# Eight prompt heads and a gelu: wider value tiles, the mask last, GpSimd for the division

## The reference

```python
z = rms_norm(x) @ w_in                      # inputs of three mixers and their gates
y_rg = RG-LRU(z)                            # conv, gates, scan
q = norm(cq @ w_uq);  latent, k_pe = ...    # 8 heads, 64 + 32 (rotary), latent of 256
s = (q_nope . k_nope + q_pe . k_pe) * ATTN_SCALE
p = softmax(where(mask, s, NEG_INF));  y_at = p @ v      # v of 64 columns a head
y_cm = gelu(u) * (w_s @ layer_norm(gelu(v)) + b_s)       # chunks of 128 tokens
x = x + (sum of gates * (y @ w_branch)) @ w_out
x = x + (silu(hf @ w_gate) * (hf @ w_up)) @ w_down
```

## Time and profile before

| | us |
|---|---|
| median of three runs | 1579.99 (1579.91 to 1580.33) |
| the profiled execution | 1581.96 |
| its span, from the first instruction to the last | 1580.0 |
| PE busy | 1550.8 (98%) |
| DVE busy | 1056.6 (67%) |
| ACT busy | 891.5 (56%) |
| POOL busy | 524.7 (33%) |

### The profile page before, as it was taken

One profiled execution on the slowest core, in us unless ns is written; L12 is line 12 of the kernel. 1 busy time (PEld: TensorE's weight loads), 2 busy tenths in 40 slices (PEclk: granted clock), 3 DMA queues, 4 the chain that ended last, 5 costly groups with the idle time before them and its releaser, 6 DMA issues.

```text
span 1580.0 us, 33275 instructions
## 1 busy us (share of the span) xinstructions
PE 1550.8 (98%) x10796; PEld 1507.2 (95%) x10796; DVE 1056.6 (67%) x1620; ACT 891.5 (56%) x1740; POOL 524.7 (33%) x709
## 2 busy tenths in 40 slices
PE   7999999999999999999999999999999999999999
PEld 7987999999999999999998789999999999999999
DVE  6777767776664766664376877777775658666633
ACT  5787776777533444443357877677764335444432
POOL 3723377676600000000048224777766001000000
PEclk9999999999999999999999999999999999999999
DMA  7331454553645444444454224545436444444443
GB/s 277 121 102 51 117 171 145 147 149 104 187 132 156 148 146 149 152 153 146 146 189 130 77 66 118 179 141 153 139 117 178 138 157 147 147 146 148 155 148 113
DMA packets 114722, 224.65 MB, mean 142 GB/s; under 512 B 12881, under 2 KB 78706, under 8 KB 114482
## 3 DMA queue, kind: packets, MB, share of 16 engines
q1 hardware_dynamic: 112178, 214.75, 44.1%
q0 software_dynamic: 2432, 8.49, 1.6%
HBM read 220.73 MB, written 2.46 MB: 141 GB/s over the span
## 4 chain that ended last, share of the span: by engine, by line
PE 81%; DVE 5%; ACT 4%; issue 3%; POOL 2%; POOLq 2%; DVEq 2%; ACTq 1%; DMA 0%; SPq 0%
PE PS L820 53%; PE PS L1075 20%; DVE w_lo L1768 1%; PE PS L1105 1%; PE PS L1106 1%; POOL r_lo L751 1%; ACT w_hi L1321 1%; POOLq L724 1%; DVEq L1762 1%; ACT r_hi L1321 1%; PE PS L876 1%; ACT lt_hi L1321 1%; PE PS L847 1%; POOL q_rot L711 0%; DVEq L2049 0%
## 5 line engine op out<-in xcount | busy, mean ns | idle before, releaser
L1768 DVE TENSOR_TENSOR w_lo<-raw,w_hi 128x1024 fp32r<-128x1024 f32 x258 | 324.9, 1260 | 221.3 <-ACT w_hi L1321 218.4
L1321 ACT ACTIVATE w_hi<-raw 128x1024 fp32r<-128x1024 f32 x258 | 272.2, 1056 | 348.6 <-PE PS L820 334.4
L820 PE MATMUL PS<-h_hi,w_hi 128*128 128x320 f32 x1360 | 425.9, 313 | 11.2 <-DVE h_lo L1795 10.4
L820 PE MATMUL PS<-h_lo,w_hi 128*128 128x320 f32 x1360 | 420.8, 309 | 0.0
L820 PE MATMUL PS<-h_hi,w_lo 128*128 128x320 f32 x1360 | 420.7, 309 | 0.0
L820 PEld LDWEIGHTS PS<-h_hi,w_hi 128*128 128x128 f32 x1360 | 255.9, 188 | 14.6 <-issue 9.6
L820 PEld LDWEIGHTS PS<-h_lo,w_hi 128*128 128x128 f32 x1360 | 256.0, 188 | 1.0
L820 PEld LDWEIGHTS PS<-h_hi,w_lo 128*128 128x128 f32 x1360 | 255.9, 188 | 0.0
L1321 ACT ACTIVATE ksqp<-PS 128x512 f32<-128x512 f32 x256 | 152.6, 596 | 135.4 <-PE PS L1075 131.6
L2109 DVE TENSOR_REDUCE kss<-ksqp 128x8 f32<-128x512 f32 x256 | 173.2, 680 | 80.5 <-ACT ksqp L1321 79.8
L1075 PE MATMUL PS<-comb_hi,lt_hi 128*128 128x288 f32 x1024 | 224.0, 300 | 3.0 <-DVE lt_lo L1771 1.5
(11 more groups left out here) (325 smaller groups left out, 2683.8 us busy)
## 6 DMA issues: line engine op xcount, KB each, us to landing
raw<-in_stream SPq DMA_DIRECT2D x258, 512.0 KB, 3.5
tpage<-in_tcache SPq DMA_DIRECT2D x256, 160.0 KB, 2.3
rrow<-in_rcache SPq DMA_DIRECT2D x256, 128.0 KB, 2.7
x<-in_xT SPq DMA_DIRECT2D x2, 640.0 KB, 7.0
sbias<-in_sbias POOLq DMA_DIRECT2D x2, 640.0 KB, 6.5
out_yT<-x SPq DMA_DIRECT2D x4, 320.0 KB, 2.2
const<-in_consts SPq DMA_DIRECT2D x1, 1090.0 KB
wgate<-in_wgate POOLq DMA_DIRECT2D x2, 512.0 KB, 4.4
```

The source lines that it names most:

```text
L820: done = mm(out, w[:, slot, c], a, start=first and n == 0 and m == 0, stop=last and n == len(pairs) - 1 and m == 2)
L1321: return nc.scalar.activation(out, in_, func, **kw)
L1768: V.tensor_tensor(w_lo[:, s, :], raw[:, s, :], f(w_hi[:, s, :]), ALU.subtract).then_inc(lo_done.sem, 1)
```

## The change

In one edit:

- The values `vp` are two tiles with 128 columns a head, 64 of them the head's and 64 zeros, placed so that a product fills all 128 partitions of the bank and two heads add up in it. GpSimd writes the zeros; ACT copies the values around them. `vp_second` lies where `wv` is loaded later, so `wv` is loaded by SyncE after `p_free`, under its own signal.
- The mask is the last product of a head's scores and covers the two diagonal tiles alone (256 columns by a repeated operand of 128).
- SCALE is in the query norms; the maxima are reduced with `negate=True`, so the multiplication by -SCALE goes, and the exponentials take no scale.
- GpSimd divides by the sums: DVE makes the reciprocal, GpSimd the two multiplications (`normalised`), with its own copying of queries between the heads.
- The square of `ua` is made by GpSimd ahead of the heads, in ACT's place; the gelu argument, tanh, the two halves, the gating and y2's parts are moved into pages 1 to 11 of the first sequence, on the same engines as before.
- The two affine selects of `snew` are moved into that sequence as well (`c == 1` and `c == 3`), and the wait for y2 with the block of `p_free` from `c == 2` to `c == 6`, ahead of the queries.
- hlast, convn and vrows are sent by SyncE, y1 and y2 swap places in memory, the spatial sums are made in two halves, and the order of some steps of ACT and DVE follows.

```diff
@@ gpsimd
+            nc.gpsimd.memset(by_half(vp_first)[:, :, 1:3], 0.0)
             nc.gpsimd.tensor_copy(comb_hi[:, :, :, 32:288], wk_raw[:])
...
+            pool.wait_ge(z_scaled.sem, z_scaled.at(l, 17))
+            pool.wait_ge(var_mm.sem, var_mm.at(l, 1))
+            nc.gpsimd.tensor_tensor(ge[:], ua[:], ua[:], ALU.mult).then_inc(gsq.sem, 1)
             pool.wait_ge(y0_ready.sem, y0_ready.at(l, 1))
+            nc.gpsimd.memset(by_half(vp_second)[:, :, 1:3], 0.0)
+            def normalised(h):
+                s, cols = h % 3, pst[:, h % 3, :]
+                pool.wait_ge(ps_inv.sem, ps_inv.at(l, h + 1))
+                nc.gpsimd.tensor_scalar(sp_[:, s, 0:128], sp_[:, s, 0:128], cols[:, 6:7], None, ALU.mult)
+                nc.gpsimd.tensor_scalar(sp_[:, s, 128:384], sp_[:, s, 128:384], cols[:, 7:8], None, ALU.mult).then_inc(ps_prob.sem, 1)
...
-                    if c == 2 and isinstance(b, int) and b == 0:
+                    if c == 1 and isinstance(b, int) and b == 0:
+                        pool.drain()
+                        new_scores_masked()
+                        pool.drain()
+                    if c == 3 and isinstance(b, int) and b == 0:
+                        other_sequences_masked()
+                        pool.drain()
+                    if c == 6 and isinstance(b, int) and b == 0:
                         pool.wait_ge(y2_ready.sem, y2_ready.at(l, 1))
@@ tensor
-                mm(PS[:, b, 0:384], ident_r[:], mask_r[:], start=True, stop=False)
-                for qt, c0, n in ((0, 0, 128), (1, 128, 256)):
+                for qt, c0, n in ((1, 128, 256), (0, 0, 128)):
...
+                diagonal = PS[:, b, 0:384].rearrange("p (n k) -> p n k", n=3)[:, 0::2]
+                mm(diagonal, ident_r[:], mask_r[:].rearrange("p (o k) -> p o k", o=1).to_broadcast([128, 2, 128]),
+                   start=False, stop=True).then_inc(ps_mm.sem, 1)
...
-                o = PS[64 * (h % 2):64 * (h % 2) + 64, ob, :]
-                mm(o[:, 0:256], vp[:, 0, 64 * h:64 * h + 64], pT[:, h % 2, 0:256], start=True, stop=False)
-                mm(o[:, 128:256], vp[:, 1, 64 * h:64 * h + 64], pT[:, h % 2, 256:384], start=False, stop=True).then_inc(ps_pv.sem, 1)
+                cols = slice(128 * h, 128 * h + 128)
+                mm(PS[:, ob, 0:256], vp[0][:, cols], pT[:, h % 2, 0:256], start=h % 2 == 0, stop=False)
+                mm(PS[:, ob, 128:256], vp[1][:, cols], pT[:, h % 2, 256:384], start=False, stop=h % 2 == 1).then_inc(ps_pv.sem, 1)
@@ scalar
-            A(ge[:], ua[:], ACT.Square).then_inc(gsq.sem, 1)
...
+                if not tail and p == 2:
+                    act.wait_ge(garg.sem, garg.at(l, 2))
+                    A(ge[:], ge[:], ACT.Tanh, scale=GELU_C).then_inc(gth.sem, 1)
...
+                if not tail and p == 8:
+                    act.wait_ge(sgu_y.sem, sgu_y.at(l, 2))
+                    A(y2_hi[:], ge[:], ACT.Copy).then_inc(y2h.sem, 1)
@@ vector
-                V.tensor_reduce(cols[:, 0:1], PS[:, h % 2, 0:128], AX.X, ALU.max)
-                V.tensor_reduce(cols[:, 1:2], PS[:, h % 2, 128:384], AX.X, ALU.max)
-                dve.drain()
-                V.tensor_scalar_mul(cols[:, 2:4], cols[:, 0:2], -SCALE).then_inc(ps_max.sem, 1)
+                V.tensor_reduce(cols[:, 0:1], PS[:, h % 2, 0:128], AX.X, ALU.max, negate=True)
+                V.tensor_reduce(cols[:, 1:2], PS[:, h % 2, 128:384], AX.X, ALU.max, negate=True).then_inc(ps_max.sem, 1)
...
+                if not tail and p == 1:
+                    dve.wait_ge(gsq.sem, gsq.at(l, 2))
+                    V.scalar_tensor_tensor(ge[:], ge[:], GELU_A, ua[:], ALU.add, ALU.mult).then_inc(garg.sem, 1)
+                if not tail and p in (3, 4):
+                    spatial_gelu(l, slice(2 * p - 6, 2 * p - 4))
+                if not tail and p in (6, 7):
+                    spatial_gated(l, slice(2 * p - 12, 2 * p - 10))
+                if not tail and p in (10, 11):
+                    part = slice(2 * p - 20, 2 * p - 18)
                     dve.wait_ge(y2h.sem, y2h.at(l, 1))
                     done = lo(y2_lo[:, part], ge[:, part], y2_hi[:, part])
```

More of the change, by code:

```diff
@@ L675, in _ @@
[L675 to L682, removed]
@@ L700, in queries, with place_low @@
                     nc.gpsimd.tensor_copy(comb_hi[:, k, :, q0:q0 + 32], src)
[L701 to L706, removed]
+            def place_low(b, par):
+                q0 = 0 if par else 288
                 for k in range(2):
@@ L710, in queries, with rope_parts, rope_high, rope_low @@
                                             f(comb_hi[:, k, :, q0:q0 + 32]), ALU.subtract)
+            quarter = cst("quarter").rearrange("p (v o) -> p v o", o=1).to_broadcast([128, 4, HT])
+            def rope_parts(b, par):
+                each = q128[:, bass.ds(b, 1), :].to_broadcast([128, 4, HT])
+                return each, *(q_rot[par][:, i].rearrange("p (v c) -> p v c", v=4) for i in range(2))
+            def rope_high(b, par):
+                each, hi_, _ = rope_parts(b, par)
+                nc.gpsimd.tensor_tensor(hi_, each, quarter, ALU.mult)
+            def rope_low(b, par):
+                each, hi_, lo_ = rope_parts(b, par)
                 nc.gpsimd.tensor_tensor(lo_, each, f(hi_), ALU.subtract)
-                pool.drain()
+            def rope_mask(b, par):
+                _, _, lo_ = rope_parts(b, par)
                 nc.gpsimd.tensor_tensor(lo_, f(lo_), quarter, ALU.mult).then_inc(qc.sem, 1)
-            queries(0, 0)
+            normalised(0)
+            normalised(1)
+            pool.wait_ge(abs_ready.sem, abs_ready.at(l, 1))
+            pool.sem_inc(waits_passed, 1)
+            place_high(0, 0)
+            normalised(2)
+            pool.drain()
+            place_low(0, 0)
+            normalised(3)
+            pool.wait_ge(q128_ready.sem, q128_ready.at(l, 1))
+            pool.sem_inc(waits_passed, 1)
+            rope_high(0, 0)
+            normalised(4)
+            pool.drain()
+            rope_low(0, 0)
+            normalised(5)
+            pool.drain()
+            rope_mask(0, 0)
+            normalised(6)
+            normalised(7)
             def rotary_lo(b, c):
@@ L777, in sequence @@
                             pool.sem_inc(waits_passed, 1)
-                        queries(b + 1, 1 - par)
+                        place_high(b + 1, 1 - par)
+                        rope_high(b + 1, 1 - par)
+                        pool.drain()
+                        place_low(b + 1, 1 - par)
+                        rope_low(b + 1, 1 - par)
+                        pool.drain()
+                        rope_mask(b + 1, 1 - par)
             pool.wait_ge(ps_pv.sem, ps_pv.at(l, H))
@@ L950, in spatial_and_attention_inputs @@
             pe.wait_ge(wv_in.sem, wv_in.at(l, 16))
-            for c, b in ((0, 7), (1, 0)):
+            for c, b in ((0, 0), (1, 7)):
                 pe.wait_ge(bank_free[b].sem, banks.take(l, b))
@@ L1612, in seq_exp @@
                 act.wait_ge(p_split.sem, p_split.at(l, b * 4))
-            A(prob[:], nope(par), ACT.Exp, scale=SCALE)
-            A(snp_hl[:, 0:HT], snp[:], ACT.Exp, scale=SCALE)
-            A(snp[:], snp[:], ACT.Exp, scale=SCALE).then_inc(s_exp.sem, 1)
+            A(prob[:], nope(par), ACT.Exp)
+            A(snp_hl[:, 0:HT], snp[:], ACT.Exp)
+            A(snp[:], snp[:], ACT.Exp).then_inc(s_exp.sem, 1)
         def sequence(l, b, par, tail=True, last=False):
@@ L1962, in spatial_sums @@
             dve.wait_ge(small_in.sem, small_in.at(l, 64))
-            dve.wait_ge(rows_sent.sem, rows_sent.at(l, 16))
-            V.tensor_tensor(va[:], PS[:, 4:8, 0:T], sbias[:], ALU.add)
-            for b in range(4, 8):
-                release(b)
+            dve.wait_ge(rows_sent.sem, rows_sent.at(l, 48))
+            for g in (0, 2):
+                V.tensor_tensor(va[:, g:g + 2, :], PS[:, 4 + g:6 + g, 0:T], sbias[:, g:g + 2, :], ALU.add)
+                release(4 + g)
+                release(5 + g)
         def spatial_gelu(l, g):
@@ L2117, in sequence @@
                     split(l, U_D + p // 4 - 1)
-                if not tail and p == 7:
+                if not tail and p == 12:
                     dve.wait_ge(sn_ready.sem, sn_ready.at(l, 1))
```

153 lines of the change are left out of this document (73 added, 80 removed).

## The result

The changed kernel takes 1589.14 us (median of four, 1587.73 to 1590.15), the kernel before on the same chip 1580.16; the ratio is 1.0052, with a 95% interval of 1.0037 to 1.0067. It is slower by 0.5%, where no measurable change was forecast (1582.0), and above the range (1586). The profiled execution took 1588.56 us.

What follows compares the result with a forecast made beforehand. TensorE, busy 98% of the span, was taken as the bound. Heads -1.65, gelu in pages +1.5 and queries +1.15 sum to +1.0 us a layer, +2.0 on 1579.99: 1582.0 us, range 1575.0 to 1586.0.

Steps and rivals of the forecast that it cites:

- values and mask: Prompt heads: narrower values products and a smaller mask save PE time, -1.4 us a layer, bounds 0 and -2.3.
- DVE relieved in the heads: Prompt heads: with less DVE work, the 1.08 us idle before the first values product goes (-1.1), plus 0.2 of gaps.
- kT held by the square: Before the heads: GpSimd's square holds DVE's kT product 2 us, costing +1.05 us a layer, bounds 0 and +1.65.
- division on GpSimd: Prompt heads: GpSimd's two multiplications take 0.85 us a head; cost 0, or +0.7 if they take 1.5.
- gelu in the pages: First sequence's pages: added ACT and DVE gelu work and affine selects cost +1.5 us a layer, from +0.5 to +3.
- queries behind the release: Before sequence 1: the p_free block ahead of the queries delays them 1.3 us, costing +1.15 us a layer.
- issues on the queues: Transfer queues: output transfers and the wv load moved to SyncE's queue, and zeros written by GpSimd, cost nothing.
- The PE work of a head covers it, except for the last two heads: Prompt heads: about 2.65 us of PE work a head hides GpSimd's longer chain; only the last two transposes wait, 1.4 us.
- the rival that had 1.5 us: Prompt heads: GpSimd's normalisation takes 1.5 us a head, heads gain 1.0 only, +1.65 a layer, 1583.3 us; chance 0.08.
- DVE gets 26.0 of 27.10 us: First sequence's pages: 4.7 us of gelu work raises DVE's busy time from 21.3 to 26.0 us of 27.10.
- two ACT stalls of the forecast: First sequence's pages: ACT's table load with tanh leaves PE 0.5 us short at page 5, split plus y2 copy 0.45 at page 11.
- DVE becomes the bound: Rival, sequence 0: DVE's work plus waits under affine selects exceeds 27.1 us; +2.5 us a layer, 1585.0 us; chance 0.24.

Runs made afterwards that it cites:

- e2: Changed kernel with the division by the sums back on DVE for all heads, none on GpSimd; 1582.05 us.
- e12: Changed kernel with the gelu's square back on ACT, behind the values copies; 1590.00 us, one execution.
- e6: Changed kernel with only the block of p_free moved behind the queries of sequence 1; 1586.63 us.
- e7: Changed kernel with the second gelu back in the prompt heads and DVE dividing by the sums; 1578.30 us.
- e8: Changed kernel with the gelu and both affine selects back in the heads, DVE dividing, and the square on ACT; 1579.40 us.
- e9: Changed kernel with DVE dividing by the sums for heads 6 and 7 alone; 1586.00 us.
- e14: Changed kernel, DVE dividing, selects and gelu through its halves in the heads, gating at pages 0 and 2, y2's copy at page 6, queries earlier; 1574.27 us.
- e3: Changed kernel leaving out DVE's gelu argument and four halves in the pages, signals kept; 1589.57 us, one execution.
- e4: Changed kernel leaving out ACT's gelu tanh and its table load in the pages, signals kept; 1586.75 us, one execution.
- e5: Changed kernel leaving out both DVE's gelu argument and halves and ACT's tanh with table load; 1584.78 us, one execution.
- e15: Like e14, but only gelu argument and tanh in the heads, DVE's four halves on even pages, y2's copy behind page 8's split; 1577.74 us.

## Why the prediction was wrong

| term, us a layer | forecast | measured | from |
|---|---|---|---|
| values and mask | -1.4 | -1.7 to -2.4 | PE busy, 26.76 to 25.05 here and 24.37 in e2 |
| DVE relieved in the heads | -1.3 | -2.0 to -2.7 | the rest: e2's -3.3 is the row above + 1.13 + this |
| kT held by the square | +1.05 | +1.13 | e12 |
| division on GpSimd | 0 | +2.81 | e2 |
| heads | -1.65 | -0.49 | after |
| gelu in the pages | +1.5 | +3.1 | 4.00 - 0.92 |
| queries behind the release | +1.15 | +0.92 | e6 |
| sum | +1.0 | +3.5 | |

Two layers make 7.0. From the first matmul to the end of the span the profiled executions differ by 8.45 us (1570.40 and 1578.85). The other 1.4 lie behind sequence 0: 1.23 in layer 1 and 0.20 in layer 2. Of the 1.23, 0.70 stand in layer 2's projection, where PE waits 1.27 us instead of 0.56 before the last products of `xc` and `wgate`; the rest was not traced to an instruction. The two rows at the top are one measurement and a remainder: only their sum, -4.4, is measured. The prediction also took the second layer's heads for as long as the first's; they took 28.97 us in the kernel before, with a wait of 0.86 instead of 1.08 us before the first values product.

- **Values, mask, kT and queries: right**, in mechanism and nearly in size; no run parts the issues on the queues. kT was held 1.5 us, not 2, and its 1.13 us show only as long as the gelu is out of the heads (e7 and e8 are equal). The kT row, 2.97 us instead of 1.49, agrees with what the Trainium skill, SBUF — State Buffer, § Who interferes with whom, states of a DVE instruction with two SBUF inputs beside a GpSimd one that reads SBUF.
- **"The PE work of a head covers it, except for the last two heads" failed.** Of the 2.81 us, e9 puts 1.05 on the last two and 1.76 on the six before. The price was wrong too, 1.54 us where 0.85 was taken with 1.5 as the upper bound, but the rival that had 1.5 us charged it only 0.65 a layer. The nearer row was the slow one: 0.44 us for 64 columns with a column operand, not the cast of the earlier trace rows. The 1.8 cycles an element at best of the Trainium skill, GPSIMD Engine Reference, § 3.1, had led to an estimate of 0.58 us plus dispatch; the 1.54 us of the trace do not agree with that. The same section's rule to keep elementwise work on DVE holds here, at 0.55 us.
- **"DVE gets 26.0 of 27.10 us", taken as room, failed, and the gelu in the pages was under-sized by half.** The upper bound, 3 us, was about what it cost. The two ACT stalls of the forecast, 0.5 us at page 5 and 0.45 at page 11, are there: against the same products of e14, where PE never waits, they put PE 0.63 us (e3) and 0.61 us (e5) back. What had no price is DVE's queue. Its gelu work puts PE 1.05 us back by page 10 without the tanh (e4), and behind each ACT block a low half comes late as well: 0.35 us at page 8 in e3, 0.57 at page 12 in e5. The affine selects, priced at 0.5, cost nothing with the gelu in the heads (e7 and e8). "DVE becomes the bound" comes near in time, but is not the cause by itself: leaving out DVE's work alone gives back only 0.42 us, also because PE then meets the stalls at y2's copy sooner (pages 11 to 15 cost 1.6 us in e3 and 1.2 in the kernel after).
- About 1.5 us of the 3.1 are left with both taken out (e5 less the queries' 0.92). They stand at pages 11, 12 and 14, at y2's copy behind the weight split and at low halves late behind it; e14, with the copy at page 6, has none of them.
- **DVE's relief** was under-sized, and hid part of the division's price: values, mask and relief gave 1.7 us more than forecast, the division took 2.8. That the heads missed by only 1.16 us is luck.

## What to carry to other kernels

An engine that is moved work to is priced by its slowest near row, and its place in the chain by every iteration that hands over, not by the last two. Before two stretches are compared, compare their granted clock: e3's 0.04 us was 0.42. The busy share of a helper says little about what more work costs: 3.3 us of DVE's gelu on even pages cost nothing up to y2's copy (e15), 4.7 us on odd and even ones cost 1.05 (e4). Read at which page TensorE waits, and what stands ahead in the queue of the engine it waits for. Share long work over stages by what each has room for (e14), and keep a block off the places where another stands ahead of an operand that TensorE waits for.

## What the hardware did that was not expected

In e3, e4 and e12 TensorE's clock fell in layer 1 just behind the heads' last waits (1.12 and 0.82 to 0.84 us), in e6 and e12 in layer 2 at the same place; the same waits in both layers of the kernel after did not bring it about. The windows from the last transposes to the first page, e12's and then that of the kernel after (granted clock third from the end):

```profile
133.34:136.12 2.78, 2.78 (x11) 2.41 (x12) 0.42 (x1) 0.87 (x2) 0.00 (x0) 0.57 0.00 0
```

```profile
134.59:136.39 1.80, 1.80 (x11) 1.58 (x12) 0.20 (x1) 0.88 (x2) 0.00 (x0) 1.00 0.00 0
```

0.57 is a mix of the full 2.4 GHz and the lower 1.2 GHz, and costs 1 us there. It reaches into the first page, which takes 2.14 us in e12, 2.06 in e3 and 1.95 in e4, instead of 1.67. It made single executions of these kernels hard to compare by their times, and a stretch by its length. On GpSimd, 128 columns with a column operand took 0.61 us and 256 took 0.93, where DVE took 0.29 and 0.35.
